# mLSTM stage: per-head rows of three heads spread by transfers, and a head's normalisation moved into the next head

## The reference

```python
b = cumsum(logsigmoid(f))                 # per head, over the 512 tokens
a = i - b                                 # i: input gate
m = max(0, running maximum of a)          # "maxima", one row of 512 per head
w[s, t] = (q_t . k_s) * DK**-0.5 * exp(a[s] - m[t])      # s <= t
num = sum_s w[s, t] * v_s ;  den = sum_s w[s, t]
h = num / max(|den|, exp(-(m + b)))       # "floor", one row of 512 per head
h = h * rsqrt(mean(h * h) + EPS) * mlstm_norm_g          # per head and token
y_a = sigmoid(o) * h                      # o: eight chunks of 128 channels
```

## Time and profile before

| | |
|---|---|
| median of three runs | 2920.5 us (2914.2 to 2920.52) |
| the profiled execution: its own time, and its span | 2924.76 us, 2923.0 us |
| TensorE busy | 2857.9 us, 98% of the span |
| granted TensorE clock, mean | 0.989 |
| the stage, first output chunk to first matmul of the merge | 2059.25 to 2187.26 us from the span's start |

### The profile page before, as it was taken

How to read it: one execution, slowest core, us unless ns; L and a number is a source line. 1 busy time by engine, 2 the same in 40 slices (tenths; PEclk the granted TensorE clock), 3 DMA queues, 4 the chain that set the end, 5 groups by cost and what they waited for, 6 DMA issues and landing times.

```text
span 2923.0 us, 30152 instructions
## 1 busy us (share of the span) xinstructions
PE 2857.9 (98%) x12002; PEld 2057.1 (70%) x12002; DVE 1345.0 (46%) x2510; ACT 493.0 (17%) x1075; POOL 792.7 (27%) x668
## 2 busy tenths in 40 slices
PE   8999999999999999999999999998999999999997
PEld 4655555555876378866888886775448866888873
DVE  7656565566137343325332336217455324544443
ACT  2100000012125153113100002005331001000011
POOL 1234343332212001421344440110014412544420
PEclk9999999999999999999999999999999999999998
DMA  6334333341100100221222221210012222222211
GB/s 241 119 109 139 94 122 112 90 152 58 49 25 9 51 1 30 87 95 42 101 87 87 87 87 58 79 68 16 29 43 87 87 82 79 91 87 87 87 53 62
DMA packets 51755, 231.69 MB, mean 79 GB/s; under 512 B 4256, under 2 KB 10784, under 8 KB 38176
## 3 DMA queue, kind: packets, MB, share of 16 engines
q1 hardware_dynamic: 40960, 181.17, 18.1%
q0 software_dynamic: 9072, 39.85, 4.3%
q10 hardware_dynamic: 1584, 8.75, 0.8%
HBM read 227.66 MB, written 2.10 MB: 79 GB/s over the span
## 4 chain that ended last, share of the span: by engine, by line
PE 92%; DVE 5%; ACT 1%; DMA 1%; issue 1%; POOL 0%; DVEq 0%; ACTq 0%
PE banks L649 60%; PE banks L585 19%; PE banks L776 2%; PE banks L799 2%; PE banks L1015 1%; PE banks L930 1%; PE banks L1023 1%; PE banks L594 1%; DVE banks L2069 1%; PE banks L1208 1%; PE banks L943 1%; DVE scratch_b L1758 1%; DMA residual<-xT 0%; PE banks L1016 0%; PE banks L1192 0%
## 5 line engine op out<-in xcount | busy, mean ns | idle before, releaser
L649 PE MATMUL banks<-big 128*128 128x256 f32 (+1 forms) x2240 | 572.2, 403 | 0.0
L2456 POOL TENSOR_TENSOR big<-weight_ring 128x512 f32<-128x512 f32 (+2 forms) x117 | 141.1, 1206 | 1446.1 <-PE banks L649 746.1
L649 PEld LDWEIGHTS banks<-big 128*128 128x128 f32 x2240 | 424.9, 190 | 112.8 <-DVE rpb_rows L1852 2.5
L649 PE MATMUL banks<-big,weight_ring 128*128 128x256 f32 (+1 forms) x1504 | 398.2, 409 | 3.3 <-DVE scratch_a L1858 2.6
L649 PEld LDWEIGHTS banks<-big,weight_ring 128*128 128x128 f32 x1504 | 285.3, 190 | 87.8 <-DVE scratch_a L1858 3.8
L649 PE MATMUL banks<-normed,weight_ring 128*128 128x256 f32 (+1 forms) x1312 | 342.6, 404 | 2.1 <-ACT rstd L1665 1.3
L585 PE MATMUL banks<-normed,weight_ring 128*128 128x256 f32 (+4 forms) x944 | 307.4, 484 | 1.2 <-ACT normed L1298 0.6
L649 PEld LDWEIGHTS banks<-normed,weight_ring 128*128 128x128 f32 x1312 | 249.1, 190 | 69.6 <-ACT rstd L1665 2.1
L585 PEld LDWEIGHTS banks<-normed,weight_ring 128*128 128x128 f32 (+2 forms) x944 | 177.8, 189 | 123.9 <-issue 108.2
L2457 POOL TENSOR_TENSOR big<-weight_ring 128x512 f32<-128x512 f32 (+2 forms) x142 | 210.8, 1485 | 0.0
L649 PE MATMUL banks<-normed,big 128*128 128x256 f32 (+1 forms) x840 | 203.7, 389 | 0.0
(11 more groups left out here) (426 smaller groups left out, 3458.2 us busy)
## 6 DMA issues: line engine op xcount, KB each, us to landing
weight_ring<-weights SPq DMA_DIRECT2D x144, 1024.0 KB, 4.8
rpb_rows<-w_ada POOLq DMA_DIRECT2D x28, 512.0 KB, 3.9
p_embed<-w_ada POOLq DMA_DIRECT2D x28, 512.0 KB, 3.9
weight_ring<-weights SPq DMA_DIRECT2D x16, 768.0 KB, 4.4
weight_ring<-weights SPq DMA_DIRECT2D x14, 512.0 KB, 3.3
weight_ring<-weights SPq DMA_DIRECT2D x8, 640.0 KB, 3.7
big<-w_ada POOLq DMA_DIRECT2D x2, 2048.0 KB, 8.3
residual<-xT ACTq DMA_DIRECT2D x2, 1536.0 KB, 12.2
```

What stands on the lines that cost most here:

```text
L649: last = nc.tensor.matmul(z, stationary(p), moving(p), start=opens and p == 0, stop=p == kp - 1, skip_group_check=True)
L2456: T(w[2], a11, a21, ALU.subtract).then_inc(sums_c, 1)
```

## The change

- Gate columns and head 0's two products with `select` are put among the second output chunk's matmuls (after k = 3 and k = 5). The same products of heads 1 to 3 are gone, and so are their waits and the idle products of head 3.
- ACT makes, on the four rows only, minus the maxima (`ROWS` row 0) and the floors' exponentials (`ROWS` row 1). POOL issues six transfers, from one partition of these rows to all 128 partitions of a buffer, for heads 1 to 3: 512 floats to each partition, 256 KB a transfer. All six count on one semaphore, `rows_spread`, and before head 1 DVE and ACT both wait until it is 96, which is all six.
- The buffers are `MINUS_M[h]` and `FLOOR[h]`, different for each head; `rs` keeps the root alone.
- The first two diagonal blocks and exponentials of a head are put at the end of the head before. The root's reciprocal of head h - 1 stands after the fourth diagonal block of head h, and its two products after head h's fourth block of weights. On ACT the root of a head stands behind the next head's first two pairs of exponentials.
- The squares go to `TMP5` in place of `SQ5`.

```diff
+        MINUS_M = [rs[:, 0:S], ROWS[:, 5, :], OG[6], OG[7]]
+        FLOOR = [SQ5[:, 2, :], big[:, 19472:19984], big[:, 19984:20496], bm_t[:, :]]
...
             og_chunk(0)
-            og_chunk(1)
...
-            pe.wait_ge(gate["ready"], 1)
+            og_chunk(1, {4: gate_columns, 6: first_rows})
             for h in range(X_HEADS):
-
-                if h >= 1:
-                    pe.wait_ge(ml["floor"], h)
-                    pe.wait_ge(ml["root"], h)
-                nc.tensor.matmul(bank[:, 0, :], con("select", h * P, P, 4), ROWS[0:4, 3, :], start=True, stop=True)
-                nc.tensor.matmul(bank[:, 1, :], con("select", h * P, P, 4), ROWS[0:4, 4, :], start=True,
-                                 stop=True).then_inc(ml["bcast"], 1)
...
-                            if h == X_HEADS - 1:
-                                turn_over(5, still, 4)
...
                 og_chunk(OG_AFTER[h])
+                if h >= 1:
+                    pe.wait_ge(ml["root"], h)
                 for v in range(2):
                     pe.wait_ge(ml["sq"], 2 * h + v + 1)
-                    last = nc.tensor.matmul(bank[:, 0, :], ones, SQ5[:, v, :], start=(v == 0), stop=(v == 1))
+                    last = nc.tensor.matmul(bank[:, 0, :], ones, TMP5[:, v, :], start=(v == 0), stop=(v == 1))
...
             og_rows(0)
+            act.wait_ge(gate["rows"], 1)
+            A(ROWS[0:4, 0, :], ROWS[0:4, 3, :], ACT.Copy, scale=-1.0)
+            A(ROWS[0:4, 1, :], ROWS[0:4, 4, :], ACT.Exp, scale=-1.0).then_inc(gate["soft"], 1)
+            act.wait_ge(ml["bcast"], 1)
+            act.wait_ge(gate["ready"], 1)
+            A(MINUS_M[0], bank[:, 0, :], ACT.Copy, scale=-1.0).then_inc(ml["minus_m"], 1)
...
+                if h < X_HEADS - 1:
+                    og_rows(OG_AFTER[h])
+                    if h == 0:
+                        act.wait_ge(rows_spread, 96)
+                    decay(h + 1, 0)
+                    decay(h + 1, 1)
                 act.wait_ge(ml["ssq"], h + 1)
+                if h >= 1:
+                    act.wait_ge(ml["head"], h)
                 A(rs[:, 0:S], bank[:, 0, :], ACT.Sqrt, bias=eps, scale=1.0 / X_DV).then_inc(ml["root"], 1)
...
+            for h in range(X_HEADS):
+                weights_of(h, 0)
+                diagonal(h, 2)
+                weights_of(h, 1)
+                diagonal(h, 3)
+                if h >= 1:
+                    inverse_root(h - 1)
+                weights_of(h, 2)
+                weights_of(h, 3)
+                if h >= 1:
+                    normalised_head(h - 1)
...
+                if h < X_HEADS - 1:
+                    if h == 0:
+                        dve.wait_ge(rows_spread, 96)
+                    else:
+                        dve.wait_ge(ml["w"], 4 * h + 4)
+                    diagonal(h + 1, 0)
+                    diagonal(h + 1, 1)
+            inverse_root(X_HEADS - 1)
+            normalised_head(X_HEADS - 1)
...
+            pool.wait_ge(gate["soft"], 2)
+            pool.wait_ge(asw["oc"], 8)
+            for h in range(1, X_HEADS):
+                for row, spread in ((0, MINUS_M), (1, FLOOR)):
+                    pool.dma_start(spread[h], ROWS[h:h + 1, row, :].unsqueeze(1).to_broadcast([1, P, S])).then_inc(rows_spread, 16)
             pool.wait_ge(ml["used"], 4 * X_HEADS)
```

More of the change, by code:

```diff
@@ L438, in build @@
         gen = st("mla_gen", "kr", "kr_roped", "q", "qc", "rot", "q_roped", "k", "kc", "v", "vc")
-        mrg1, mrg2 = stages(2, "merge", "done", "gate", "free")
+        mrg1, mrg2 = stages(2, "merge", "gate", "free")
+        rows_spread = sem("head_rows_spread")
         ple = st("ple", "done", "gate", "free")
@@ L1155, in _, with og_chunk @@
             attention(asw, 32, sw_scores, sw_pieces, sw_values, asw["max"], (4, 5), 2, 4, 1)
-            def og_chunk(b):
+            def og_chunk(b, within={}):
                 at = 4 + b if b < 2 else 7
@@ L1166, in og_chunk @@
                 for k in range(KC):
+                    if k in within:
+                        within[k]()
                     last = mm(bank[:, at, :], slot(n, ((b % 2) * KC + k) * P, P), H[:, k, 0:S], k == 0,
@@ L1169, in og_chunk, with gate_columns, maxima_rows, floor_rows @@
                 last.then_inc(og["done"], 1)
-            og_chunk(0)
-            og_chunk(1)
[L1173 to L1178, removed]
-            pe.wait_ge(gate["ready"], 1)
-            for h in range(X_HEADS):
-                if h >= 1:
-                    pe.wait_ge(ml["floor"], h)
-                    pe.wait_ge(ml["root"], h)
-                nc.tensor.matmul(bank[:, 0, :], con("select", h * P, P, 4), ROWS[0:4, 3, :], start=True, stop=True)
-                nc.tensor.matmul(bank[:, 1, :], con("select", h * P, P, 4), ROWS[0:4, 4, :], start=True,
-                                 stop=True).then_inc(ml["bcast"], 1)
+            def gate_columns():
+                pe.wait_ge(asw["oc"], 8)
+                pe.wait_ge(gate["rows"], 1)
+                for c in range(4):
+                    last = nc.tensor.transpose(bank[:, 7, c * 4:(c + 1) * 4], ROWS[0:4, 2, c * P:(c + 1) * P],
+                                               con("ident", 0, 4, 4))
+                last.then_inc(gate["cols"], 1)
+            def maxima_rows(h):
+                nc.tensor.matmul(bank[:, 0, :], con("select", h * P, P, 4), ROWS[0:4, 3, :], start=True,
+                                 stop=True).then_inc(ml["bcast"], 1)
+            def floor_rows(h):
+                nc.tensor.matmul(bank[:, 1, :], con("select", h * P, P, 4), ROWS[0:4, 4, :], start=True, stop=True)
+            def first_rows():
+                pe.wait_ge(gate["ready"], 1)
+                maxima_rows(0)
+                floor_rows(0)
+            og_chunk(0)
+            og_chunk(1, {4: gate_columns, 6: first_rows})
+            for h in range(X_HEADS):
                 for c in range(5):
@@ L1640, in _, with decay @@
             og_rows(0)
+            act.wait_ge(gate["rows"], 1)
[4 more added lines that the diff above has]
+            A(MINUS_M[0], bank[:, 0, :], ACT.Copy, scale=-1.0).then_inc(ml["minus_m"], 1)
+            act.wait_ge(ml["minus_m"], 1)
+            def decay(h, c):
+                act.wait_ge(ml["diag"], 4 * h + c + 1)
+                if c < 3:
+                    A(SQ5[:, c % 2, P:S - c * P], MINUS_M[h][:, (c + 1) * P:S], ACT.Exp, bias=ACOL[:, c, h:h + 1])
+                A(SQ5[:, c % 2, 0:P], SQ5[:, c % 2, 0:P], ACT.Exp, bias=ACOL[:, c, h:h + 1]).then_inc(ml["e"], 1)
+            decay(0, 0)
             og_rows(1)
+            decay(0, 1)
             for h in range(X_HEADS):
[L1643 to L1654, removed]
+                decay(h, 2)
+                decay(h, 3)
                 for b in OG_WITHIN[h]:
                     og_rows(b)
-                act.wait_ge(ml["w"], 4 * h + 4)
-                A(SQ5[:, 2, :], bank[:, 1, :], ACT.Exp, scale=-1.0).then_inc(ml["floor"], 1)
+                if h == 0:
+                    act.wait_ge(ml["w"], 4)
+                    A(FLOOR[0], bank[:, 1, :], ACT.Exp, scale=-1.0).then_inc(ml["floor"], 1)
                 act.wait_ge(ml["used"], 4 * h + 4)
@@ L1662, in _ @@
                     act.wait_ge(ml["num"], h + 1)
-                    A(SQ5[:, v, :], YA[:, 2 * h + v, :], ACT.Square).then_inc(ml["sq"], 1)
+                    A(TMP5[:, v, :], YA[:, 2 * h + v, :], ACT.Square).then_inc(ml["sq"], 1)
+                if h < X_HEADS - 1:
[4 more added lines that the diff above has]
+                    decay(h + 1, 1)
                 act.wait_ge(ml["ssq"], h + 1)
+                if h >= 1:
+                    act.wait_ge(ml["head"], h)
                 A(rs[:, 0:S], bank[:, 0, :], ACT.Sqrt, bias=eps, scale=1.0 / X_DV).then_inc(ml["root"], 1)
-                og_rows(OG_AFTER[h])
-                if h < X_HEADS - 1:
-                    act.wait_ge(ml["head"], h + 1)
+            og_rows(OG_AFTER[-1])
             def output_gates():
@@ L2354, in _ @@
             V.tensor_copy(ACOL, bank[:, 7, 0:16].rearrange("p (c h) -> p c h", c=4)).then_inc(gate["ready"], 1)
[L2355 to L2379, removed]
@@ new lines, in diagonal, with weights_of @@
+            def diagonal(h, c):
+                if c >= 2:
+                    dve.wait_ge(ml["w"], 4 * h + c - 1)
+                V.tensor_tensor(SQ5[:, c % 2, 0:P], MINUS_M[h][:, c * P:(c + 1) * P], con("causal", 0, P),
+                                ALU.add).then_inc(ml["diag"], 1)
+            def weights_of(h, d):
+                dve.wait_ge(ml["e"], 4 * h + d + 1)
+                dve.wait_ge(ml["s"], 4 * h + d + 1)
+                if 4 * h + d >= 2:
+                    dve.wait_ge(ml["used"], 4 * h + d - 1)
+                V.scalar_tensor_tensor(TMP5[:, d % 2, 0:S - d * P], bank[:, 2 + d % 2, 0:S - d * P], X_DK ** -0.5,
+                                       SQ5[:, d % 2, 0:S - d * P], ALU.mult, ALU.mult).then_inc(ml["w"], 1)
@@ L2380, in _, with inverse_root, normalised_head @@
```

(18 more changed lines are left out.)

## The result

| | before | after |
|---|---|---|
| median of the timed runs | 2920.24 us (2914.03 to 2920.52, 5 runs) | 2932.04 us (2931.2 to 2932.86, 5 runs) |
| profiled execution: own time, span | 2924.76, 2923.0 us | 2932.86, 2931.1 us |
| first output chunk to merge | 128.0 us | 136.8 us |

The changed kernel is slower by half a per cent: ratio 1.005, 95% interval 1.004 to 1.0061. The forecast was 2930 (2890 to 2940), with 0.42 for faster, 0.38 for slower and 0.20 for no difference that can be told.

A forecast was written before the change was run, and what follows sets the result against it. TensorE's waits and half clock between heads were taken as the reducible 32 of the stage's 128.0 us; 26.5 us saved and 36.4 lost to late transfers gave 2920.5 + 9.9 = 2930 us, range 2890 to 2940.

The forecast's parts named there:

- The limit of the reads: Six transfers for heads 1 to 3: reads pass one partition's door at 26.6 GB/s, 59.1 us, landed at 2133.7.
- One semaphore for six: Before head 1: one semaphore counts all six transfers, so head 1 waits for head 3's rows; 36.4 us lost.
- The last harmless moment: Before head 1's values: transfers landed by 2098.3 cost nothing; every microsecond beyond counts in full.
- The gain of the order: Heads 0 to 3, if transfers land in time: 4.7 + 10.0 + 6.3 + 5.5 = 26.5 us saved.
- The clock: TensorE: full clock in head 0; 0.50 after the stall before head 1's values, first block 4.15 us instead of 2.57.
- a wrong step: Signs against the forecast's steps: clock at 0.50 in head 0, or head 3's third block waiting for the reciprocal.
- The third block of head 3: Head 3, no chunk as cover: reciprocal ends just when this block needs its weights; up to 2 us could show.
- The merge: End of the stage, after head 3: begins at 2197.2, 9.9 us later than before.
- The range: Whole kernel: 2890 to 2940 us, taking in hidden transfers and the forecast's spread, leaving out the slowest case and tails.
- the hidden case: Rival, transfers before head 1: sixteen engines read in parallel, landing before 2098.3; 26.5 us saved, 2894 us; chance 0.34.
- the two bounds: Landing of the six transfers: 2078.3 if sixteen engines read side by side, 2133.7 through one partition's door.
- the slow one: One partition's door for the six transfers, 59.1 us, head 1 stalled: 2925 to 2938 us; chance 0.48.

The follow-up runs named there:

- the three transfers: Changed kernel with the three floors not transferred, so half the bytes, and the common wait at 48: 2901.01 us (one run), stage 107.6 us.
- the second profile of before: The kernel before, unchanged, profiled again: 2920.5 us, 126.6 us from first output chunk to merge.

## Why the prediction held, step by step

- **The limit of the reads** held in its place and its size: the source's side, 27 to 28 GB/s for an estimate of 26.6, and a last landing at 2131.7 for 2133.7. Its grounds held only in part. The rate was taken from one of sixteen engines that queue at one partition; the experiments show a door that four neighbouring partitions share. Why its rate should be that of one engine no run shows, so the closeness of the number is in part luck. The nearest row by size and queue, 3.9 us for 512 KB, would have misled.
- **One semaphore for six** held: head 1 waited for head 3's floor, and splitting the wait gave back 34 us, where 36.4 were foreseen as lost, with a landing 2 us later than it came.
- **The last harmless moment**, 2098.3, is 39 us behind the first output chunk. The runs enclose it: the pair that head 1 waits for landed 35.2 us behind that chunk (2092.67) and cost nothing, the three transfers landed 43.3 us behind it (2101.05) and cost the stage 4.4 us, 2.5 of them idle.
- **The gain of the order**, 26.5 us, was slightly too large: 24.8 us from stage to stage. Head 0's values ended at 2084.99 instead of 2083.95. The scores began 0.8 us later than forecast, since instructions of 512 columns in short groups took more than 0.428 us (groups of four between two changes of kind 1.83 to 1.92 us from start to start, not 1.71), and the first weights waited for the score until 2076.95. Later heads took 24.33 for 24.2 and head 3 18.0 for 17.6.
- **The clock** held in kind: 0.50 after the stall, where the first block took 4.59 us and not 4.15, and 1.00 in head 0, where a fall would have been a sign of a wrong step. The third block of head 3 did not wait for the reciprocal either.
- **The merge** began at 2196.2, 8.9 us later than before; 9.9 were forecast, 11.8 came out between the medians. The other 3 us come from the profiled executions: that of before was 4.5 us above its median of 2920.24 and that of after 0.8 above its own, and behind the merge the changed kernel took 0.8 us less. Against the second profile of before (2183.75) the merge is 12.4 us later.
- **Not foreseen**: SP's load of 1 MB, issued at 2086 beside the transfers, landed 48.9 us later instead of 4.8. No engine waited for it in this kernel or in the one with one semaphore a head, where it took 49.0. With a ring of fewer slots it could have been a second stall; no run shows that.
- **The range** held the time, but from 2890 to 2940 it takes in a gain of 30 us as well as a loss of 20 and would have held for the hidden case too. What was at stake is the choice between the two bounds, taken at 0.48 for the slow one against 0.34 for the hidden one. By the verdicts faster was even a little ahead, 0.42 against 0.38. Nothing in the trace of before could have narrowed this, since no row there reads one partition from all engines.

## What to carry to other kernels

A broadcast out of one partition is priced by the source's door and not by the number of DMA engines: here 27 GB/s, 9.6 us for 256 KB, so that the six transfers of 1.57 MB needed some 60 us of cover from the first issue to the last landing. Where the cover was there, the transfers cost nothing that showed and took work from TensorE. Wait for each when it is needed, not for all when the first is. And an operation between two stretches of work is worth moving where no other work covers it: one head in four gave 85% of what the move was worth.

## What the runs showed of the hardware

- Sixteen DMA engines can show a busy share of 0.96 at 27 GB/s, where 1.01 went with 426 GB/s elsewhere: the share tells of waiting as well as of moving, and only with GB/s beside it can the two be told apart.
- Slow transfers held up another on the same engines: a load of weights issued beside the six took 48.9 us, where such loads take 4.8 alone. Its 1 MB moved only when the six were through, at 178 GB/s from 2130 to 2136, with 27 to 28 GB/s in all before. SP's loads in the changed kernel, from 2050 to 2200:
```profile
DMA to landing us min/median/max: 4.8/4.9/48.9
```
- An issue from ACT's queue blocked ACT for up to 9.6 us when earlier transfers stood in the queue; from POOL six issues took 0.54 us each.
- Changing the activation table took 1.30 us from the start of the load to the next activation, and the load began at once behind the activation before it. ACT's timeline of the changed kernel:
```profile
2134.99 0.69 ACT L1691 ACTIVATE rstd<-banks,params_sb 128x512 f32<-128x512 f32 x1
2135.70 1.28 ACT L1663 ACT_TABLE_LOAD   x1
2137.00 0.40 ACT L1663 ACTIVATE scratch_a<-big 128x128 f32<-128x128 f32 x1
```
The Trainium skill, "ScalarE: Activation LUTs", What ACT_TABLE_LOAD costs, gives 2.66 us for such a change, 1.283 for the load and 1.38 for a drain. The trace agrees with the load, 1.28 us, and not with the sum: no drain shows in these rows.
